# Interleaved decoder trunk: first tiles of each layer split and summed differently, and stick-breaking attention walked in 32 two-head steps

## The reference

```python
for i in range(DEPTH):
    h = rms_norm(x, norm_g[i])
    x = x + mixer[i % 3](h)        # A: DeltaNet, B: stick-breaking, C: short conv

def stick_breaking_mixer(h, w_in, q_norm_g, k_norm_g, w_out):
    q, k, v, gate = jnp.split(h @ w_in, 4, axis=-1)
    q, k = rms_norm(q, q_norm_g), rms_norm(k, k_norm_g)       # per head: 16 heads of 64
    z = einsum('bqhd,bshd->bhqs', q, k) * scale
    mask = key_pos < q_pos
    log1m = where(mask, -softplus(z), 0)
    after = cumsum(log1m, reverse=True) - log1m
    wts = where(mask, exp(log_sigmoid(z) + after), 0)
    o = einsum('bhqs,bshd->bqhd', wts, v)
    return (o * silu(gate)) @ w_out
```

## Time and profile before

| | us |
|---|---|
| median of 3 runs (lowest to highest) | 1921.04 (1919.13 to 1921.28) |
| profiled execution | 1917.61 |
| its span, first to last instruction | 1915.8 |
| PE busy | 1834.7 (96%) |
| DVE busy | 875.6 (46%) |
| ACT busy | 841.4 (44%) |
| POOL busy | 611.4 (32%) |
| mean granted TensorE clock | 0.99 |

### The profile page before, as it was taken

The page is one execution under the profiler, slowest core; times in us unless marked ns, Lnnn a source line. Parts: engine busy times, 40 slices in busy tenths (PEclk is TensorE's granted clock), DMA queues, the critical chain, the costliest instruction groups (busy, mean ns, idle before and its releaser), DMA issues.

```text
span 1915.8 us, 23158 instructions
## 1 busy us (share of the span) xinstructions
PE 1834.7 (96%) x8864; PEld 1474.9 (77%) x8864; DVE 875.6 (46%) x1314; ACT 841.4 (44%) x1195; POOL 611.4 (32%) x154
## 2 busy tenths in 40 slices
PE   5999989999998999999999999999989998899999
PEld 4688778878887666658878888888867887888787
DVE  7665944243241444443573443333166577443410
ACT  5575333585232565663432222222256734237721
POOL 3333310233333010102434443443433233013342
PEclk9999999999998999999999999999999999999999
DMA  4122210022321101012222223222222133001222
GB/s 173 66 88 89 97 46 12 24 90 88 108 88 66 45 22 44 25 41 67 88 88 97 100 88 109 88 97 100 88 88 88 66 88 116 12 7 67 88 100 76
DMA packets 46977, 144.66 MB, mean 76 GB/s; under 512 B 28080, under 2 KB 28208, under 8 KB 30768
## 3 DMA queue, kind: packets, MB, share of 16 engines
q1 hardware_dynamic: 46896, 143.55, 22.4%
HBM read 138.29 MB, written 5.24 MB: 75 GB/s over the span
## 4 chain that ended last, share of the span: by engine, by line
issue 63%; PE 21%; POOL 14%; DVE 1%; SPq 0%; POOLq 0%; ACT 0%; DMA 0%; DVEq 0%
POOL w_lo L396 14%; PE ps L1479 4%; PE ps L1481 4%; PE ps L1480 4%; PE ps L1725 3%; PE ps L1778 1%; PE ps L1773 1%; PE ps L1735 1%; PE ps L1764 1%; PE ps L1751 1%; PE ps L1685 1%; PE ps L1699 0%; DVE k_out L1197 0%; PE ps L1827 0%; POOLq L401 0%
## 5 line engine op out<-in xcount | busy, mean ns | idle before, releaser
L396 POOL TENSOR_TENSOR w_lo<-w_raw,w_hi 128x2048 fp32r<-128x2048 f32 x126 | 585.2, 4644 | 1083.0 <-ACT w_hi L464 1083.0
L1479 PE MATMUL ps<-h_hi,w_hi 128*128 128x512 f32 x1488 | 600.0, 403 | 39.7 <-POOL w_lo L396 27.2
L1480 PE MATMUL ps<-h_lo,w_hi 128*128 128x512 f32 x1488 | 583.7, 392 | 0.0
L1481 PE MATMUL ps<-h_hi,w_lo 128*128 128x512 f32 x1488 | 583.5, 392 | 0.0
L1479 PEld LDWEIGHTS ps<-h_hi,w_hi 128*128 128x128 f32 x1488 | 282.2, 190 | 111.4 <-POOL w_lo L396 30.6
L1480 PEld LDWEIGHTS ps<-h_lo,w_hi 128*128 128x128 f32 x1488 | 282.1, 190 | 61.3 <-issue 4.6
L1481 PEld LDWEIGHTS ps<-h_hi,w_lo 128*128 128x128 f32 x1488 | 281.8, 189 | 60.3
L464 ACT ACTIVATE w_hi<-w_raw 128x2048 fp32r<-128x2048 f32 x126 | 240.4, 1908 | 129.6 <-PE ps L1481 123.4
L1479 PE MATMUL ps<-y_hi,w_hi 128*128 128x512 f32 x448 | 174.3, 389 | 0.0
L1480 PE MATMUL ps<-y_lo,w_hi 128*128 128x512 f32 x448 | 174.3, 389 | 0.0
L1481 PE MATMUL ps<-y_hi,w_lo 128*128 128x512 f32 x448 | 174.3, 389 | 0.0
(11 more groups left out here) (182 smaller groups left out, 2336.3 us busy)
## 6 DMA issues: line engine op xcount, KB each, us to landing
w_raw<-w_tiles SPq DMA_DIRECT2D x126, 1024.0 KB, 4.9
x<-x_t SPq DMA_DIRECT2D x4, 512.0 KB, 9.2
out_t<-x SPq DMA_DIRECT2D x8, 256.0 KB, 5.4
scr_u<-lt SPq DMA_DIRECT2D x8, 128.0 KB, 2.7
u_blk<-scr_u SPq DMA_DIRECT2D x2, 512.0 KB, 3.3
scr_v<-v_blk SPq DMA_DIRECT2D x2, 512.0 KB, 2.6
scr_t<-v_t SPq DMA_DIRECT2D x2, 512.0 KB, 3.6
d_g<-scr_t SPq DMA_DIRECT2D x32, 32.0 KB, 2.0
```

Of the source, the lines that this page charges most:

```text
L396: pool.tensor_tensor(w_lo[:, slot, :], w_raw[:, slot, :], w_hi[:, slot, :].bitcast(F32), ALU.subtract).then_inc(lo_done, 1)
L1479: pe.matmul(out_, w_h, m_h, start=start, stop=False)
L1480: pe.matmul(out_, w_h, m_l, start=False, stop=False)
L1481: return pe.matmul(out_, w_l, m_h, start=False, stop=stop)
```

## The change

1. **Split of x.** `gain_x` is gone. ACT rounds x with the gain as its scale, and DVE makes the low part with one instruction out of x, gain and `h_hi`.
2. **Layer 0.** ACT squares the even blocks, DVE the odd ones, into a buffer of eight (`sq8`), and PE sums all eight over partitions with ones-matmuls, four beside the last blocks of tile 0 and four behind it.
3. **Half a first tile.** Of the DeltaNet layers' first tiles (`ab_tiles`) only 128 of 256 channels are loaded, rounded and subtracted (`w_part`).
4. **Low parts.** DVE makes those of tiles 0, 1 and of the third tile of every layer (at block 3 of `norm`), and of the stick-breaking tiles t0 + 7 to t0 + 13. POOL makes the others.
5. **Norm of stick-breaking.** The turned 1/rms is made at block 1 of the second tile instead of 4, and the first tile is scaled at block 5 instead of after all blocks.
6. **DeltaNet.** The exponentials on the decay rates come behind the first `tap`.
7. **Stick-breaking.** The two heads of a pair go together through 4 steps, 32 in all. z of both, then both masks, two projection blocks, sums (steps 1 and 3), pv of two steps before for both heads, one block, cum of the step before for both, one block. Eight blocks lie ahead of the first step, so the projection runs on into the first gate tile. From that tile on the bank order is turned by one.
8. **Loops** over output steps are written out on ACT and DVE.

```diff
+    def unrolled(first, n, step):
+        for k in range(n):
+            step(first + k, 0, k)
...
     def bank(s, c):
-        return ps[2 * (s % 2) + c]
+        return ps[2 * ((s + (s >= turn)) % 2) + c]
+    turn = tile_base[layers.index(SB)] + 12
+    def w_part(w, t):
+        if t in ab_tiles:
+            return w[:, t % 2, :].rearrange("p (k n) -> p k n", n=2 * P)[:, :, 0:P]
+        return w[:, t % 2, :]
+    def z_bank(g, e):
+        return ps[2 + 2 * (g % 2) + e]
...
+        def start_lows(l):
+            t = tile_base[l]
+            if l:
+                for q in (t, t + 1):
+                    pool.wait_ge(hi_done, q + 1)
+                    pool.tensor_tensor(w_part(w_lo, q), w_part(w_raw, q), w_part(w_hi, q).bitcast(F32), ALU.subtract)\
+                        .then_inc(lo_done, 1)
+            pool.wait_ge(lo_done, t + 3)
...
+            elif kind == SB:
+                t0 = tile_base[l]
+                lows(t0 + 3, 4)
+                pool.wait_ge(lo_done, t0 + 14)
+                pool.wait_ge(b["spl"], 6 * SB_PAIRS)
+                lows(t0 + 14, TILES[kind] - 14)
...
         def round_x(l, m, i=0, per=1):
-            act.activation(h_hi[:, m + 2 * per * i, :], hf[:, m % 2, :], ACT.Copy).then_inc(hhi_done, 1)
+            act.activation(h_hi[:, m + 2 * per * i, :], x[:, m + 2 * per * i, :], ACT.Copy, scale=g).then_inc(hhi_done, 1)
...
                     tap(j, c)
+                    if x_ == 0:
+                        decay_exps()
...
+            for j in range(SB_PAIRS):
+                more = j + 1 < SB_PAIRS
+                for v in range(4):
+                    g = 4 * j + v
+                    softplus(g)
+                    if more and v in (0, 2):
+                        square_qk(j + 1, v // 2)
+                    if more and v in (1, 3):
+                        rms_qk(j + 1, v // 2)
+                    if g:
+                        weights(g - 1)
+                    if v == 2:
+                        hi(t0 + 7 + j)
...
         for m in range(KD):
             act.wait_ge(x_loaded[m // 2], 16)
             round_x(0, m)
-            square_x(0, m)
-            if m == 1:
+            if m % 2 == 0:
+                act.activation(sq8[:, m, :], x[:, m, :], ACT.Square).then_inc(sq0_even, 1)
+            if m == 0:
                 hi(0)
...
+            dve.scalar_tensor_tensor(h_lo[:, k, :], x[:, k, :], g, h_hi[:, k, :].bitcast(F32), ALU.mult, ALU.subtract)\
                 .then_inc(h_done, 1)
...
+                if k == 3:
+                    low_w(t0 + 2)
+                if k == 5 and kind == SB:
+                    dve.wait_ge(turned_rstd, 1)
+                    dve.tensor_copy(bexp[:, 0:NB], ps[6][:, 0:NB]).then_inc(rstd_tok, 1)
+                    dve.wait_ge(rstd_tok, 1)
+                    scale_v(l, t0)
...
+            for j in range(SB_PAIRS):
+                more = j + 1 < SB_PAIRS
+                for v in range(4):
+                    if more and v in (0, 2):
+                        raw_qk(j + 1, v // 2)
+                    softplus(4 * j + v)
+                    if v == 0 and j:
+                        low_w(t0 + 6 + j)
+                    if more and v in (1, 3):
+                        scaled_qk(j + 1, v // 2)
+                    if v == 2 and j:
+                        evac(j - 1)
+                    if v == 2 and more:
+                        values(j + 1)
...
         for m in range(KD):
             dve.wait_ge(x_loaded[m // 2], 16)
-            gain_x(0, m)
-            if m:
-                low_x(0, m - 1)
-                sum_squares(0, m - 1)
-        low_x(0, KD - 1)
+            low_x(0, m)
+            if m == 0:
+                low_w(0)
+            if m % 2:
+                dve.tensor_tensor(sq8[:, m, :], x[:, m, :], x[:, m, :], ALU.mult).then_inc(sq0_odd, 1)
+        low_w(1)
...
+                if l == 0 and k >= 4:
+                    sum_first(k - 4)
...
+            if l == 0:
+                for m in range(4, KD):
+                    sum_first(m)
...
-                if k == 4 and midway:
+                if k == 1 and midway:
...
+            def z(g):
+                for e in range(2):
+                    rr = slice(64 * e, 64 * e + 64)
+                    pe.matmul(z_bank(g, e)[:, 0:w], sb_qk[rr, j % 2, 1, kb * P:kb * P + P], sb_qk[rr, j % 2, 0, kb * P:T],
+                              start=True, stop=False, skip_group_check=True)
+                for e in range(2):
+                    pe.matmul(z_bank(g, e)[:, 0:P], cb[:, B_ID:B_ID + P], cb[:, B_STRICT:B_STRICT + P],
+                              start=False, stop=True, skip_group_check=True).then_inc(b["z"], 1)
+            def pv(g):
+                for e in range(2):
+                    own = slice(64 * e, 64 * e + 64)
+                    pe.matmul(ps[6 + j % 2][own, kb * P:T], sb_v[:, j % 2, kb, own], sb_w[:, e, 0:w],
+                              start=(kb == 3), stop=(kb == 0), skip_group_check=True).then_inc(b["pv"], 1)
+            fill(16)
+            sums(0, 0)
+            sums(0, 1)
+            fill(8)
+            for j in range(SB_PAIRS):
+                more = j + 1 < SB_PAIRS
+                for v in range(4):
+                    g = 4 * j + v
+                    z(g)
+                    fill(2)
+                    if more and v in (1, 3):
+                        sums(j + 1, v // 2)
+                    if g >= 2:
+                        pv(g - 2)
+                    fill(1)
+                    if g:
+                        cum(g - 1)
+                    fill(1)
```

More of the change, by code:

```diff
@@ L725, in stickbreak @@
             walk(act, t0, 4, v_step)
[L727 to L766, removed]
-            hi(t0 + 5)
[L769 to L791, removed]
+            def square_qk(p, c):
+                act.wait_ge(b["raw"], 2 * p + c + 1)
+                if p:
+                    act.wait_ge(b["ss"], 2 * p + c - 1)
+                act.activation(sb_sq[:, c, :], sb_raw[:, c, :], ACT.Square).then_inc(b["sq"], 1)
@@ new lines, in weights @@
+            def weights(g):
+                w = P * (g % 4 + 1)
+                for e in range(2):
+                    act.wait_ge(b["cum"], 2 * g + e + 1)
+                    if g:
+                        act.wait_ge(b["pv"], 2 * g + e - 1)
+                    act.activation(sb_w[:, e, 0:w], z_bank(g, e)[:, 0:w], ACT.Exp).then_inc(b["w"], 1)
+            hi(t0 + 5)
+            square_qk(0, 0)
+            square_qk(0, 1)
+            hi(t0 + 6)
+            rms_qk(0, 0)
+            rms_qk(0, 1)
@@ L801, in gate_step @@
             def gate_step(t, i, k):
-                if not (isinstance(i, int) and k == 0):
+                if k > 1:
                     hi(t + 1, i)
@@ L1950, in stickbreak @@
-            parts = [(c, k) for c in range(2) for k in range(KD)]
-            share = [4, 4, 4, 4]
-            def pair(j, i, first, last):
-                t = t0 + 4 + j
-                rest = list(parts)
-                for u in range(8):
-                    z(u, j, i)
-                    if not last:
-                        if u == 0:
-                            qk_ready(t + 1, i)
-                        if u < len(share):
-                            for _ in range(share[u]):
-                                qk_part(t + 1, i, *rest.pop(0))
-                    if not (first and u < 2):
-                        cum(8 * j + u - 2, i)
-                    if not (first and u < 3):
-                        pv(8 * j + u - 3, i)
-                    if u == 5 and not last:
-                        sums(j + 1, i)
@@ new lines, in stickbreak, with fill @@
+            blocks = 16 * (SB_PAIRS + 1)
+            done = [0]
+            def fill(n):
+                for _ in range(n):
+                    if done[0] < blocks:
+                        project(done[0])
+                        done[0] += 1
+            fill(16)
[10 more added lines that the diff above has]
+                        sums(j + 1, v // 2)
+                    if g >= 2:
+                        pv(g - 2)
+                    fill(1)
+                    if g:
+                        cum(g - 1)
+                    fill(1)
```

368 lines of the change are left out of this document (179 added, 189 removed).

## The result

The changed kernel takes 1863.7 us (median of 4 runs, 1862.7 to 1864.4), the kernel before 1921.2 in the runs beside it: ratio 0.970, 95% interval 0.9685 to 0.9718. The step that fell short is the overlap of the two heads' matmuls on the halves of the array, taken at one pass where two overlap. The profiled execution took 1864.35 us.

A forecast was written before the change was run, and what follows sets the result against it. PE, busy 96% of the span, was taken as the bound. Terms -3.6 - 9.2 - 21.2 - 3.3 - 4.4 = -41.7 took the profiled 1917.6 us to 1875.9; with 3.4 for the median, 1879, range 1867 to 1899.

The forecast's parts named there:

- Term 3: Stick-breaking pairs: cheaper shape changes and one overlapping pass per couple, less a new wait; -21.2 us, -6.3 without overlap.
- the coupling: Stick-breaking: issuing both heads of a step together needs fewer openings and closings of array shapes, saving 1.35 us per pair.
- The new wait: Stick-breaking pair border: next scores wait 1.1 us for scaled keys, made behind the widest step's ACT and DVE instructions.
- the ends and the clock: Stick-breaking: projection blocks before first scores -1.5, last pair with half the gate tile -0.9, half clock at 616 -2.0.
- Term 1: Start of the kernel: half tile and DVE low part start PE earlier, fourth tile at 52.6, clock drop charged; -3.6 us.
- Term 2: Start of stick-breaking: the third tile's 5.8 us wait goes, with 3.4 us of half-clock loss; -9.2 us.
- Term 4: Short-conv layer's second tile: chain and gap 2.4 us shorter, half clock taken at half, -0.9; -3.3 us.
- Term 5: Last layer: fourth tile's gap falls from 4.5 to 1.9 us, half the clock loss back, -1.7; -4.4 us.
- (a): Stick-breaking: the halves of the array don't overlap, so term 3 is -6.3 and the time 1894 us; chance 0.30.
- (b): Layer starts: gaps stay because another wait ends there; 1891 us with overlap, 1906 without; chance 0.09.
- (c): Stick-breaking: slower, the chain scores, ACT, DVE, cumulative sum, keys bounds a pair; 1934 us at an 8 us wait; chance 0.04.

The follow-up runs named there:

- a3: Changed kernel with both heads' score matmuls on the same array rows and both heads' value matmuls on the same array columns: 1890.5 us.
- a1: Changed kernel with both score matmuls of a step reading array rows 0 to 63, head 0's operands, each into its own bank: 1880.2 us.
- a4: Changed kernel with each head's mask issued directly behind its scores, instead of both scores and then both masks: 1882.7 us.
- b1: Changed kernel with the first taps of both halves of DeltaNet's first channel tile on ACT before the decay exponentials: 1857.6 us.
- d1: b3 with the first convolution multiplication of short-conv's first group made by ACT instead of DVE: 1847.8 us.
- a2: Changed kernel with both value matmuls of a step using head 0's weights and array columns 0 to 63: 1876.0 us.
- c1: Changed kernel with stick-breaking's first tile scaled after all eight normalized blocks again, DVE still making the third tile's low part: 1868.5 us.
- c2: Changed kernel with POOL again making the low parts of the first three tiles in the three later layers: 1867.9 us.
- c3: Changed kernel with the decay exponentials again before the first tap: 1864.2 us.
- b3: Changed kernel with the edits of b1 and b2 together: 1847.9 us.
- b2: Changed kernel with the next pair's key sums, rms pair on ACT and scaling on DVE ahead of the widest step's softplus: 1855.1 us.
- c4: Changed kernel loading, converting and subtracting the whole first tile of the DeltaNet layers instead of half: 1866.9 us.

## Why the prediction was right or wrong, step by step

**Term 3, the step that failed.** The prediction says: "PE starts matmuls in order and the second instruction's first pass has only the first's last pass to lie beside, so I take one pass per couple." Here the reasoning failed: the order is kept between instructions, but their passes alternate, so the first passes run side by side and then the second passes. A couple costs what one head costs, two passes are saved, 4.27 us per pair (a3 against the kernel after) instead of 2.13. The forecast had named two passes as the other bound and "this one pass or more" as what the Trainium skill's rule gives ("TensorEngine Tiling (Array Packing)", Key Properties: tiles work independently and a change of mode drains). a1 to a3 bear out its first half in full, and a4's 0.30 us for an opening and a closing agrees with the second. I chose the lower end from an argument about order, not from a row; no row stood behind it. The 2.13 us missed, less 0.2 for the coupling, times seven pairs are about 13.4 of the 15 us.

The other sizes of the term held. Coupling saves 1.13 us per pair (1.35 forecast). The new wait is 1.08 us in each of seven borders (1.1 forecast), by the cause named. Without overlap the pair would be 30.87 (31.0 forecast). The last pair's chain waits 1.61, 0.58 and 0.69 us, 2.9 together, where 4 was forecast. But PE ran at half clock from 809.4 to 812.8, and the second wait stands behind that. In the eight traces b1 to d1 PE is at full clock up to that wait, and the three are 1.61, 1.85 and 0.69, 4.15 together: the 4 was right. With the last pair's own couples, which overlap too, the ends and the clock gave 7.6 us, 3.2 more than the 4.4 forecast; these were not taken apart further.

**Term 1, -3.6, measured -6.7.** PE starts at 10.09, not at 11 to 12.5: the half tile had landed by 7.72, when ACT's conversion of 1.06 us began, not at 8.5 to 9.7. About one microsecond of this is chance: in a2, with the same start, the half tile landed by 8.62 and PE started at 10.99, and the eight traces with the same code that far have the fourth tile at 50.9 to 52.1. So in the trace of the kernel after 1/rms is there at 26.5 instead of 28.0, and the fourth tile starts at 51.2 instead of 52.6. The other 1.7 is the clock drop that I charged to this term; it came, for 3.4 us at 51.7, but behind the point at which the 6.7 is read.

**Term 2, -9.2, measured -7.35.** The wait of 5.8 us went for the reason given (c1, c2). The clock's part was overpriced: the half-clock stretch at 572.0 was 6.8 us long, but PE was idle until 575.98, so only 2.8 us of it slowed work, which costs 1.4 and not 3.4.

**Term 4, -3.3, measured -1.6.** The gap fell to 2.17, not 1.4, and a half-clock stretch of 3.4 us stays behind it (932.3). **Term 5, -4.4, measured -2.7.** The fourth tile's gap fell from 4.5 to 2.59 (1.9 forecast), and with a shorter wait ahead of it that tile starts 2.5 us earlier, 2.6 forecast. Before, 2.4 of the 6.8 us at half clock lay in the gap, so the stretch cost 2.2 and not 3.4; all of it came back, more than the 1.7 I took. What the forecast lacked is the next wait: the last layer now waits 1.07 us at its key norms (PE's sums of the squares `ksq`), where the trace before doesn't. In all fourteen traces this wait of 0.7 to 1.1 us is there when PE runs on at full clock behind the fourth tile (last layer: kernel after, a2, c3, b1, b3, d1; first layer: kernel before, b1, b3, d1) and absent when half clock follows that tile. So it takes back part of what a regained clock gives. The moved exponentials gave exactly their 1.0 (c3).

**What no term held.** Layer 0 behind its fourth tile gained 1.8 us (the stretch at 51.7 costs it 1.6; a wait of 1.05 at the key norms, shorter half clock near 245 and 0.6 less of a DMA wait outweigh that) and the last layer behind its starts lost 4.8, since its state part (the matmuls from 1560 us on) fell to half clock for twice 6.8 us, where the trace before has one stretch of 3.4, and waited 0.9 longer for a DMA. Nothing in the change bears on that stretch: in the other twelve traces it has 3.4 to 10.2 us of half clock, so much of this is the chance of one trace. Together -3.0. And I carried the 3.4 us between the profiled execution of before and the median of its runs over to the forecast; the profiled execution of the changed kernel lies 0.6 above its median. The ledger against 1879: term 3 16.6, term 1 3.1, terms 2, 4 and 5 -5.3, the rest of the two layers -3.0, median 4.0, sum 15.4.

**Rivals.** (a) is refuted by a3: without overlap the time is 1890.5, and the kernel took 1863.7. (b) is refuted by the waits that went, though the fourth tiles' stayed in part as feared. (c), the bound by the chain, was right in its place and cause and small in its price; b2 shows it is a matter of order on ACT and DVE.

**The range.** Its lower end took in the unknown clock but not the other bound of the overlap, although that bound was on the page: two passes give -17 more, 1862. With a bound of an unknown cost so cheap to state, the range should have reached it.

## What to carry to other kernels

Where matmuls use half of the array, issue two that use different halves directly behind one another: in this kernel two fp32 instructions of two passes each then cost what one costs, and a single full-array matmul between them loses it. When PE gets faster, look at which short instruction on ACT or DVE stands behind the widest step's work; here moving the keys' scaling (with the sums and the rms it needs) and one tap forward gave another 16 us. Removing a DVE instruction that meets POOL's long subtraction may gain nothing, since the next one can meet it, as in d1.

## What the runs showed of the hardware

Both passes of two fp32 matmuls on different halves start within 7 ns of one another, for rows with different banks (scores) and for columns with the same bank (values): 26.08 us of PE work per pair against 28.21, 28.23 and 30.35 without.

The same gap does not always bring half clock. The windows 239.90 to 246.70 and 263.80 to 267.20 hold the same code, first in the kernel after, then in a1:

```profile
239.90:246.70 6.80, 4.86 (x27) 4.63 (x28) 2.39 (x4) 4.36 (x9) 1.24 (x1) 0.75 0.55 170
263.80:267.20 3.40, 3.40 (x27) 3.25 (x26) 1.27 (x3) 1.20 (x2) 0.00 (x0) 1.00 0.00 0
```

```profile
239.90:246.70 6.80, 4.82 (x22) 4.42 (x23) 2.43 (x4) 3.59 (x6) 1.29 (x1) 0.50 0.54 170
263.80:267.20 3.40, 3.40 (x12) 2.86 (x11) 1.05 (x2) 0.60 (x1) 0.00 (x0) 0.50 0.00 0
```

The same stretch is granted 1.2 GHz for all of 6.8 us in one execution and for half of it in the other, and the second window is at full speed in one and at half in the other. The wait of 2.17 us at short-conv's second tile is followed by 3.4 us at half clock in seven of the eleven traces that have it, and by full clock in four (a2, a3, a4, c4). What PE did before them is the same: 220.04 and 220.26 us of busy time in the first 239.9. The runs of c2 differ by 9 us, those of the kernel after by 1.6, and the clock can account for it: c2's mean granted clock is 0.989 in the run of 1873.8 us and 0.994 in that of 1864.9. The difference is 0.5% of 1872 us, 9.4 us (an estimate: the clock is given to 0.001, about 2 us, and half clock in idle time costs nothing). A gain of a microsecond or two is read from the gaps of a trace, not from the time.
